# Attention by pairs of heads, with scores on row halves and values on column halves of the array

## What is computed

```python
px = modulate(rmsnorm(x, norm_mix), m3, m4) @ w_mix_in
pc = modulate(rmsnorm(ctx, norm_mix), mc3, mc4) @ w_mix_in
q, k, v, gb, gc, u = split_heads(px, q_norm, k_norm)   # rmsnorm over each head
qc, kc, vc, gbc, gcc, uc = split_heads(pc, q_norm, k_norm)
a = latent_attention(apply_rope(q, cos, sin), apply_rope(k, cos, sin), v, kc, vc)
sc = gb * short_conv3(gc * u, conv_w)
mix = concatenate([rmsnorm(a, attn_out_norm), rmsnorm(sc, conv_out_norm)])
x = x + m5 * (mix @ w_mix_out)
```

## Time and profile before

| | us |
|---|---|
| median of 3 runs | 2865.19 (2865.05 to 2865.75) |
| the profiled execution | 2861.57 |
| its span | 2859.3 |
| QKV stretch in it | 660 to 714 |
| attention stretch in it | 714 to 901 |

### The profile page before, as it was taken

The page is one execution under the profiler, slowest core; times in us unless marked ns, Lnnn a source line. Parts: engine busy times, 40 slices in busy tenths (PEclk is TensorE's granted clock), DMA queues, the critical chain, the costliest instruction groups (busy, mean ns, idle before and its releaser), DMA issues.

```text
span 2859.3 us, 37052 instructions
## 1 busy us (share of the span) xinstructions
PE 2790.1 (98%) x14453; PEld 2233.2 (78%) x14453; DVE 1489.2 (52%) x2096; ACT 1139.2 (40%) x1697; POOL 513.2 (18%) x297
## 2 busy tenths in 40 slices
PE   8999999999999999999999999999999999999999
PEld 4888888866656688887898888887868877788887
DVE  6734534257546633335754656554267775653443
ACT  4221212224444432223655555554466663432221
POOL 0000000023111100002444444434422223100000
PEclk9999999999999999999999999999999999999999
DMA  6422313143102322222211211111211112232222
GB/s 234 151 78 83 120 63 111 53 139 120 37 30 88 127 93 92 96 92 100 80 53 45 67 56 64 53 53 38 74 60 60 60 60 93 95 103 93 91 97 81
DMA packets 69871, 241.77 MB, mean 85 GB/s; under 512 B 8218, under 2 KB 8346, under 8 KB 69314
## 3 DMA queue, kind: packets, MB, share of 16 engines
q1 hardware_dynamic: 62032, 221.28, 22.9%
q10 hardware_dynamic: 7666, 18.13, 1.9%
HBM read 232.74 MB, written 6.64 MB: 84 GB/s over the span
## 4 chain that ended last, share of the span: by engine, by line
PE 87%; DVE 5%; ACT 5%; DMA 1%; issue 1%; ACTq 0%; DVEq 0%; POOL 0%; SPq 0%; POOLq 0%
PE ps L1098 61%; PE ps L1484 3%; PE ps L1288 2%; PE ps L1381 2%; PE ps L1257 2%; PE ps L1585 2%; PE ps L1421 1%; PE ps L1275 1%; PE ps L1128 1%; PE ps L1309 1%; PE ps L1413 1%; ACT r L461 1%; DVE UT L468 1%; PE ps L1266 1%; ACT w_hi L461 1%
## 5 line engine op out<-in xcount | busy, mean ns | idle before, releaser
L1098 PE MATMUL ps<-Nh,w_hi 128*128 128x512 f32 (+1 forms) x1808 | 660.5, 365 | 9.5 <-DVE Nl L468 4.9
L1098 PE MATMUL ps<-Nl,w_hi 128*128 128x512 f32 (+1 forms) x1808 | 630.0, 348 | 0.0
L1098 PE MATMUL ps<-Nh,w_lo 128*128 128x512 f32 (+1 forms) x1808 | 628.0, 347 | 0.0
L461 ACT ACTIVATE w_hi<-w_raw 128x1024 fp32r<-128x1024 f32 (+1 forms) x352 | 368.7, 1047 | 637.4 <-PE ps L1098 521.8
L468 POOL TENSOR_TENSOR w_lo<-w_raw,w_hi 128x1024 fp32r<-128x1024 f32 x125 | 308.0, 2464 | 750.4 <-ACT w_hi L461 746.7
L468 DVE TENSOR_TENSOR w_lo<-w_raw,w_hi 128x1024 fp32r<-128x1024 f32 (+1 forms) x227 | 281.8, 1242 | 257.5 <-ACT w_hi L461 247.8
L1098 PEld LDWEIGHTS ps<-Nh,w_hi 128*128 128x128 f32 x1808 | 342.6, 190 | 80.2 <-issue 30.1
L1098 PEld LDWEIGHTS ps<-Nl,w_hi 128*128 128x128 f32 x1808 | 342.7, 190 | 50.6 <-issue 5.8
L1098 PEld LDWEIGHTS ps<-Nh,w_lo 128*128 128x128 f32 x1808 | 342.4, 189 | 44.1
L1098 PE MATMUL ps<-x1h,w_hi 128*128 128x512 f32 (+1 forms) x784 | 272.3, 347 | 1.9 <-DVE x1l L479 1.9
L1098 PE MATMUL ps<-x1l,w_hi 128*128 128x512 f32 (+1 forms) x784 | 266.6, 340 | 0.0
(11 more groups left out here) (353 smaller groups left out, 4725.0 us busy)
## 6 DMA issues: line engine op xcount, KB each, us to landing
w_raw<-in_w_in SPq DMA_DIRECT2D x132, 512.0 KB, 3.5
w_raw<-in_w_proj SPq DMA_DIRECT2D x89, 512.0 KB, 3.4
w_raw<-in_w_ada SPq DMA_DIRECT2D x52, 512.0 KB, 4.1
w_raw<-in_w_out SPq DMA_DIRECT2D x48, 448.0 KB, 3.2
w_raw<-in_w_out SPq DMA_DIRECT2D x24, 512.0 KB, 3.4
w_raw<-in_w_mix_in SPq DMA_DIRECT2D x19, 512.0 KB, 3.5
w_raw<-in_w_bdn SPq DMA_DIRECT2D x16, 512.0 KB, 3.4
w_raw<-in_w_mix_out SPq DMA_DIRECT2D x8, 512.0 KB, 3.5
```

What stands on the lines that cost most here:

```text
L461: self.then_inc(self.e.activation(out, in_, func, **kw), sem)
L1098: ins = e.matmul(out[:, 512 * j:512 * j + n], a[:, kk, :], x[:, kk, c0:c0 + n], start=k == 0 and p == 0, stop=k == nt - 1 and p == 2)
```

## The change

- Units of `w_mix_in` are projected in the order 4, 0, 6, 5, 1, 2, 3; the sums and the rotation of the last (unit 3) move into the attention stretch, behind the first score and two groups.
- Rotated queries and keys are split into `qTh`, `qTl`, `kTh`, `kTl` (rounded by ACT, remainder by DVE); the root's exact step takes two DVE operations and one more square on ACT.
- A score event takes two heads that share keys, the even on rows 0 to 63 and the odd on rows 64 to 127, alternating, three fp32r products each for 512 and for 256 keys. DVE takes both maxima, then both divisions; ACT both exponentials.
- `vp` holds only the 64 columns; a value event takes 256 queries of both heads, the even head to partitions 0 to 63 and the odd to 64 to 127, alternating, f32 of 256 columns. `PT` has one set of two tiles of 256 columns.
- The convolution's copies and its first product stand at the last event of their unit; the taps wait for the next score event (`tapping`).
- All remainders of `w_mix_in` weights go to DVE. POOL no longer zeroes `vp`.

```diff
+MIX_UNITS = [4, 0, 6, 5, 1, 2, 3]
+NORMED = [4, 0, 5, 1, 2, 3]
+TURNED_OUT = [2, 3, 5, 6, 7, 8]
...
+    out = [("score", 0)]
     fills = products("w_mix_in", [7 + i for i in range(12)])
...
+    for m in range(16):
+        tiles = fills[0:8] if m == 0 else fills[6 * m + 2:6 * m + 8]
+        a, b = ("turn", 2 * m), ("turn", 2 * m + 1)
+        score = [("score", m + 1)] if m < 15 else []
+        if m == 0:
+            out += tiles[0:2] + [("ones", 5), ("rot", 5), ("vturn", 0)] + tiles[2:4] + [("vturn", 1)]
+            tiles = tiles[4:]
+        if m % 2 == 0:
+            out += [a] + score + tiles[0:2] + [b] + tiles[2:]
         else:
...
+            out += [a] + tiles[0:1] + [b] + tiles[1:2] + score + tiles[2:4] + [("value", m // 2)] + tiles[4:]
+        if m in (5, 9, 13):
+            out.append(("square", "mixc", (m - 5) // 4))
+        elif m in (6, 10, 14):
+            out.append(("square", "att", (m - 6) // 4))
+    return out
...
-_POOLED = [(split_of("w_mix_in", 4), split_of("w_mix_out", 0)),
-           (split_of("w_proj", 3), split_of("w_o2", 0))]
+_POOLED = [(split_of("w_proj", 3), split_of("w_o2", 0))]
...
+        self.qTh, self.qTl = mem.put("qTh", [P, 4, TX], F32R), mem.put("qTl", [P, 4, TX], F32R)
+        self.kTh, self.kTl = mem.put("kTh", [P, 2, T1], F32R), mem.put("kTl", [P, 2, T1], F32R)
+        self.vp = mem.put("vp", [P, 6, 2, 64])
...
-        self.PT = [mem.put(f"PT{i}", [P, 6, TX]) for i in range(2)]
+        self.PT = [mem.put(f"PT{i}", [P, 6, 2 * P]) for i in range(2)]
...
-        values = r.of["p", split_of("w_mix_in", 6)][0]
-        last, r, conv = r.last, Ring(sorted((b for b in r.order if b != 3), key=lambda b: b == values)), Ring([7])
+        final = r.of["p", split_of("w_mix_in", MIX_UNITS[-1])][0]
+        last, r, conv = r.last, Ring(sorted((b for b in r.order if b != 3), key=lambda b: b == final)), Ring([7])
         r.last.update(last)
         conv.last[7] = last[3]
-        self.of.update({("vturn", 0): (3, last[3]), ("vturn", 1): (3, (s.v_out, 4))})
...
+        self.of.update({("vturn", 0): (3, last[3]), ("vturn", 1): (3, (s.v_out, 2))})
         for ev in ATTENTION:
             if ev[0] == "score":
-                r.use(ev, s.exp, ev[1] + 1)
+                for n in (2 * ev[1], 2 * ev[1] + 1):
+                    r.use(("score", n), s.exp, n + 1)
...
+            w.wait_ge(s.q_hi, (2, 4, 5, 6)[p])
+            w.wait_ge(s.q_lo, (2, 4, 5, 6)[p])
+            outs = [pair(ps, bank_of(("score", 2 * ev[1] + x))) for x in range(2)]
             for c0, nn in COLS1:
-                ins = e.matmul(out[:, c0:c0 + nn], t.qT[r0:r0 + 64, h // 2, qb * P:(qb + 1) * P],
-                               t.kT[r0:r0 + 64, h // 4, c0:c0 + nn], start=True, stop=True)
-            w.then_inc(ins, s.score)
+                for i, (qt, kt) in enumerate(((t.qTh, t.kTh), (t.qTh, t.kTl), (t.qTl, t.kTh))):
+                    for x in range(2):
+                        rows = slice(64 * x, 64 * x + 64)
+                        ins = e.matmul(outs[x][:, c0:c0 + nn], qt[rows, p, qb * P:(qb + 1) * P],
+                                       kt[rows, p // 2, c0:c0 + nn], start=i == 0, stop=i == 2)
+                        if c0 and i == 2:
+                            w.then_inc(ins, s.score)
...
+            p, half = divmod(ev[1], 2)
+            w.wait_ge(s.pt, 8 * ev[1] + 8)
+            w.wait_ge(s.v_out, 4)
+            if half == 0:
+                w.wait_ge(s.att, p)
+            for i in range(6):
+                for x in range(2):
+                    ins = e.matmul(ps[64 * x:64 * x + 64, 6, 256 * half:256 * half + 256], t.vp[:, i, p // 2, :],
+                                   t.PT[x][:, i, :], start=i == 0, stop=i == 5)
+            w.then_inc(ins, s.value)
...
+    def head_root(n):
+
+        T = TX if NORMED[n] < 4 else T1
+        q = t.qk[n % 2]
+        w.wait_ge(s.q_mm, n + 1)
+        w.act(q[2][:, 0:T], pair(ps, B.of["ones", n][0])[:, 0:T], ACT.Ln, s.act_step, scale=1.0 / 64, bias=cs("eps", n=1))
+        w.act(q[3][:, 0:T], q[2][:, 0:T], ACT.Exp, s.act_step, scale=-0.5)
+        w.act(q[2][:, 0:T], q[3][:, 0:T], ACT.Square, s.q_exp)
+
+    def rounded(n):
+
+        i = NORMED[n]
+        w.wait_ge(s.q_out, TURNED_OUT[n])
+        dst = t.qTh[:, i, :] if i < 4 else t.kTh[:, i - 4, :]
+        w.copy(dst, t.qk[n % 2][1][:, 0:TX if i < 4 else T1], s.q_hi)
...
+    taken_in(MIX_UNITS[-1])
+    rounded(4)
...
+        if ev[0] == "score":
+            attend(2 * ev[1])
+            attend(2 * ev[1] + 1)
+        elif ev[0] == "ones":
+            head_root(ev[1])
+        elif ev[0] == "mm":
+            if ev[3] == 0:
+                highs(split_of("w_mix_in", ev[2]) - 1, last)
+            elif ev[3] == KT - 1 and (ev[2] - 7) % 3 < 2:
+                conv_in(ev[2] - 7)
         elif ev[0] == "turn":
-            if ev[1] + 1 < 32:
-                attend(ev[1] + 1)
+            turned(ev[1])
+            if ev[1] == 5:
+                rounded(5)
...
+        w.wait_ge(s.q_exp, n + 1)
+        w.stt(tt, pair(ps, B.of["ones", n][0])[:, 0:T], 64 * EPS, square, ALU.add, ALU.mult, s.q_v)
+        w.stt(y, tt, -192.0, y, ALU.add, ALU.mult, s.q_n)
...
+        w.tt(tt[:, 0:TX], rot, t.c1("sin"), ALU.mult, s.q_sin)
+        w.wait_ge(s.q_cos, n + 1)
         w.tt(v[:, 0:TX], v[:, 0:TX], tt[:, 0:TX], ALU.add, s.q_n)
-        w.tt(dst[:, 0:TX], v[:, 0:TX], y[:, 0:TX], ALU.mult, s.q_out)
-        if i >= 4:
-            w.tt(dst[:, TX:T1], raw[:, TX:T1], y[:, TX:T1], ALU.mult, s.q_out)
+        w.stt(v[:, 0:TX], v[:, 0:TX], -1.0 / 128, y[:, 0:TX], ALU.mult, ALU.mult, s.q_out)
...
+    def remainder(n):
+
+        i = NORMED[n]
+        hi, lo = (a[:, i, :] if i < 4 else b[:, i - 4, :] for a, b in ((t.qTh, t.kTh), (t.qTl, t.kTl)))
+        w.wait_ge(s.q_hi, n + 1)
+        w.tt(lo, t.qk[n % 2][1][:, 0:TX if i < 4 else T1], hi.bitcast(F32), ALU.subtract, s.q_lo)
...
+            for n in (2 * ev[1], 2 * ev[1] + 1):
+                largest(n)
+            for n in (2 * ev[1], 2 * ev[1] + 1):
+                divided(n)
+            if ev[1] == 4:
+                remainder(5)
+            if tapping is not None:
+                convolved(tapping)
+                tapping = None
+        elif ev[0] == "ones":
+            remainder(4)
+            head_root(ev[1])
+        elif ev[0] == "rot":
+            rotated(ev[1])
+        elif ev[0] == "vturn":
+            values(ev[1])
+        elif ev[0] == "mm":
+            if ev[3] == 0:
+                lows(split_of("w_mix_in", ev[2]) - 1, last)
+            elif ev[3] == KT - 1 and (ev[2] - 7) % 3 == 2:
+                tapping = (ev[2] - 9) // 3
+                conv_product(tapping)
+                if tapping == 3:
+                    convolved(tapping)
```

## The result

The changed kernel takes 2855.27 us (median of 20 runs), the kernel before 2864.97 us (20 runs): the ratio of the medians is 0.9966, that of the means (2856.88 and 2865.02 us) 0.9972 with a 95% interval of 0.9962 to 0.9981, so 0.28% faster by the means. Forecast was 2855.0. The profiled execution took 2852.99 us with a span of 2851.2 us, against 2861.57 and 2859.3.

The account below looks back on a forecast made before the run. TensorE, busy 98% of the span, bounds the kernel. Work -47, old waits -2, stalls +21 and +9, clock +9 give -10: 2861.6 to 2851.6, plus 3.6 for the median, 2855 us; 8-in-10 range 2830 to 2882.

Parts of the forecast that it names:

- TensorE's work: TensorE's own products in the attention stretch: about 47 us less, from scores (24.8) and values (22).
- Scores: Attention scores: 32 x 1.60 = 51.2 us before, 16 x 1.65 = 26.4 us after; saving 24.8 us, bounds 14 and 31.
- rival 5: Score weight loads also run side by side, piece at its lower bound: 6 us less, 2849 us; chance 0.08.
- Values: Attention values: 44.3 us before, 8 x 2.8 = 22.4 us after, side by side; saving 22 us, or 1 us taking turns.
- part 1: The scores step of the prediction, counting 0.11 us for the product behind each piece; saving 24.8 us.
- rivals 1 and 2: Halves take turns: scores and values, +27, 2882 us, chance 0.15; or only f32 values, +17, 2872 us, chance 0.12.
- rival 2: Only the f32 values take turns, weight loads under short passes: pieces 5.2 us, +17, 2872 us; chance 0.12.
- Part 3: Attention stretch: two heads' softmax in a row delays convolution copies and products; TensorE stalls at eleven unit boundaries, 21.2 us.
- Part 4: Start of attention: TensorE waits 2.5 us before the first score and 6.3 us for the value tile; together 9 us.
- The ring: DVE, ACT, DVE steps in the last query tiles: 7.4 us with gaps, against 5.5 plus 1.7 us on TensorE.
- DVE 63%, no bound: Attention stretch: with 11 us more remainders DVE is busy 104 of 165 us, so it does not bound.
- Part 5: Half clock after attention stalls: four of eight stalls, 6.8 us, plus 2.5 us behind the 6.3 us one; 9 us.

Follow-up runs that it names:

- scores_on_same_rows: Changed kernel with both heads' scores taken from rows 0 to 63; mixer's output product starts at 912.4 us, against 890.9.
- values_by_head: Changed kernel with one head's six products in each value piece issued before the other's; mixer's output product starts at 904.1 us, against 890.9.
- u_before_score: Changed kernel with the last two groups of three u units moved before the score; mixer's output product starts at 900.5 us, against 890.9.
- combined: Changed kernel with f32 scores on row halves, values turned earlier, last sums and rotation later, second gb buffer, gc copied between exponentials; 2834.33 us (median of 4).
- gc_before_score: Changed kernel with the last two groups of four gc units moved before the score; mixer's output product starts at 886.8 us, against 890.9.
- start_reordered: Changed kernel with values turned earlier, last sums and rotation later, fifth tile's remainder behind first softmax; mixer's output product at 889.9 us, against 890.9.

## Why the prediction came true, step by step

The mechanism was the one forecast: paired products, and a gain mostly given back to new waits and the lower clock. That the median came within 0.3 us of the forecast is luck: single runs of the changed kernel lie up to 18 us apart, and several terms were wrong and cancelled.

**TensorE's work: -46.8 forecast, -47.6 measured.** *Scores*, the price after, was the term most wrong: 1.65 us forecast, 1.26 and 0.11 behind it measured, 16 x 1.37 = 21.9 us against 26.4. Before, a piece was 1.48 and 0.11 by the starts, 50.9 us in all. Saving 29.0, not 24.8. I had let twelve weight loads of 0.12 us limit the piece; they do not. That was rival 5, and its reasoning held, though not its total; its chance (0.08) was too small: the Trainium skill, page "TensorE: Matmul & The Clock Gate" (Part 3, The mechanism), gives this result, and the trace agrees, with pairs at 0.23 us. *Values*: after, 2.74 and 0.10 behind, 8 x 2.84 = 22.7 us, forecast 22.4. But the price of before was too high: the chain's 1.72 and 1.91 us count the hand-over at a score that part 1 had already counted. By the starts a piece was 1.42 (behind a score, 765.32 to 766.74) or 1.32 us (742.80 to 744.12), and the product behind it lasted 0.63 us to the next start instead of 0.23: 24 x 1.72 = 41.3 us without the hand-over, not 44.3. Saving 18.6, not 22.

The weight loads of the values, in the changed kernel by form (ns shortest, median, longest; first and last start):

```profile
L1306 PEld LDWEIGHTS ps<-PT,vp x192: 132/137/137, 746.7 to 890.4; 128*64 128x64 f32 x192
```

They take 137 ns for half as many columns as the 190 ns of the earlier trace rows. 24 of them one behind the other would be 3.3 us, more than the 2.74 us of the piece, so the loads of the two halves overlap as well. With that, rivals 1 and 2 fall: scores_on_same_rows shows what turns cost the scores (2.30 us), the lone passes in values_by_head what they would cost the values (24 passes 0.22 us apart are 5.2 us), and the changed kernel pays neither. The rule on column tiling of the Trainium skill, page "TensorEngine Tiling (Array Packing)" (Restrictions), was the reason for rival 2; whether it is at work in the 137 ns no run here tells, and the piece came out at 2.74 us, not at the 5.2 us feared.

**Part 3: the stops, 21.2 us forecast, 21.5 measured.** Gc 8.8 and measured 9.7, its last being 3.56 us where 2.2 had been counted for each; gb 8.5 and measured 8.2; cu 3.9 (with 0.7 for a remainder) and measured 3.6. Each is released by what the written order gave. This counting of positions in two queues, with durations from the earlier trace rows, was the best step of the prediction.

**Part 4: the start, 9 us forecast, 9.8 measured**, but shared out otherwise: the first score waited 4.2 us, not 2.5, and the value tile 5.6, not 6.3, so the total is closer than its parts. The ring's sum (7.4 us a tile against 5.5 and 1.7 on TensorE) does not by itself give the 3.9 us by which DVE was said to end late. Not foreseen was 1.5 us in the projections for m_t on ACT. "DVE 63%, no bound" was right as a mean (103.41 of 176 us, 59%) and is of little use: u_before_score got 5.6 us of new waits from five DVE steps in the wrong place.

**Part 5: the clock, 9 us forecast, some 4.5 us by subtraction and at most 7.1.** Windows of the changed kernel (columns as in the first such view):

```profile
718.00:722.00 4.00, 3.34 (x15) 2.82 (x16) 3.26 (x6) 0.71 (x2) 1.00 (x1) 0.61 0.07 30
732.00:736.00 4.00, 3.88 (x19) 3.27 (x21) 0.78 (x3) 0.98 (x2) 0.00 (x0) 0.50 0.00 0
820.00:824.00 4.00, 2.45 (x8) 2.09 (x9) 1.00 (x2) 2.64 (x4) 0.00 (x0) 0.66 0.00 0
862.00:866.00 4.00, 3.56 (x12) 2.92 (x12) 1.23 (x1) 2.93 (x6) 0.00 (x0) 0.57 0.00 0
```

Four falls to 0.50 (1.2 GHz): two at the waits of the start and two at gb stops, each in the wait or right behind it. Of the eight stalls that I had put between 2.2 and 2.5 us I let four be followed by a fall; it was three, the first score's and two for gb. The work at full clock should be 336.2 - 47.6 + 2.9 = 291.5 us (the 2.9 in the next paragraph), it was 296.0, so 4.5 us were lost. The windows give 7.1 at most. What is measured is the sum of the clock and the 2.9 us, 7.4 us; how it divides hangs on the estimate below.

**Left out: 2.9 us.** A stop costs more than its idle time. The turning at 754.48 takes 0.57 us when something follows it at once; the next product started at 757.32, 2.27 us later than 755.05, and 2.03 is listed. The 0.24 us are the tail of the last product, which otherwise lies under the next. Some twelve stops make 2.9 us. This is an estimate from one place, not measured by a run. It has one support: combined has 295.2 us of work at full clock, and with 3.7 us for its dearer scores taken off that is 291.5 as well.

**The sum**: -47.6 + 2.9 + 4.5 + 30.7 (idle, of which 28 were forecast) = -9.5 us, against 9.4 measured at Eh and -10 forecast. By these figures I had put the scores 4.2 us too high and the clock 4.5, and had counted 3.4 us too much of saving for the values, 2.7 too little of idle and nothing for the tails (2.9): these misses cancel, so the total says less for the terms than it seems to. The medians differ by 9.7 us and the means by 8.1, as do the profiled spans, so little or nothing is left for the rest of the program.

## What to carry to other kernels

- When one engine has 98% of the span, cutting its work by 47 us shows first who was hiding under it. Take the written order, find each place at which that engine needs a bank or buffer back, and count what stands ahead of the step that frees it in the other engines' queues; here that gave 30.2 us for the stops and the start, of which 31.3 were measured (the start in other shares than forecast), and missed one wait of 1.5 us. Then remove those waits (a second buffer, one step put ahead of another), or most of the gain stays behind (here four fifths).
- Moving the waiting work elsewhere in TensorE's order gave half or more of the wait back as new ones (gc_before_score, u_before_score, start_reordered); a reordering within ACT took gc's wait from 9.7 to 4.7 us with no new one, and a second buffer gb's from some 8 to 1.0.
- Price a piece from start to start of its neighbours, and each hand-over once.

## What the runs showed of the hardware

- Two products on different rows of the array, or on different columns, run at once, f32 ones too, and so do their weight loads: 1.26 us for what takes 2.30 us on the same rows. Row halves paired even when written head by head (1.25 us); f32 passes on column halves did so only in part (4.52 us against 2.74: the second head began behind eight of the first head's twelve passes).
- A DVE division that takes 0.62 us by itself took 1.55 to 1.56 us, three times, beside a weight remainder on POOL (kernel before).
- The clock did not fall by the length of an idle alone. Timeline of TensorE in the changed kernel, four of the later waits of over 2 us (the three others are of 2.03, 2.05 and 2.28 us):

```profile
821.55 0.76 PE L1318 MATMUL ps<-x1h,w_hi 128*128 128x512 f32 x1 [2.62 <-ACT gb L463]
838.71 0.47 PE L1318 MATMUL ps<-x1h,w_hi 128*128 128x512 f32 x1 [2.07 <-ACT gc L463]
862.44 0.77 PE L1318 MATMUL ps<-x1h,w_hi 128*128 128x512 f32 x1 [2.30 <-ACT gb L463]
881.12 0.47 PE L1318 MATMUL ps<-x1h,w_hi 128*128 128x512 f32 x1 [3.56 <-ACT gc L463]
```

The first and the third (0.76 and 0.77 us for a product) came with 0.50, the fourth, the longest, did not. What decides between them is open. Runs of the changed kernel itself have a mean clock from 0.982 to 0.990, kernels with nearly the same waits from 7 to 21 us in the clock column, and combined, whose longest idle in the attention stretch is 2.1 us, none.
